# Two recurrent mixers woven on five engines: their steps re-cut so that few wait inside a step, with decays and inverse roots computed on ScalarE

## What is computed

```python
# mixer A (hgrn2), 6 heads of 64: per head, over time
G = cumsum(log_f)
o = (q * exp(G)) @ state + scores @ v         # scores: q k^T with decays exp(G_t - G_s), causal
state = exp(G_last) * state + (k * exp(G_last - G))^T @ v
y_a = rms_norm(o) * norm_w * silu(g)          # rms over the 64 of a head
# mixer B (mamba2), 6 heads of 64, 2 groups of state 128: per chunk
a_cum = cumsum(dt * a)
scores = (c b^T) * exp(segsum(dA))            # the decays of a chunk
y = scores @ xdt + exp(a_cum) * (c @ state) + d_skip * x
y_b = rms_norm(y * silu(z)) * norm_w          # rms over 192
```

## Time and profile before

| | us |
|---|---|
| median of 3 runs | 3358.85 (3358.09 to 3359.83) |
| profiled execution, its time | 3351.59 |
| its span | 3349.8 |
| the stage of both mixers, from the first fetch of their inputs (430.16) to the first product of the next stage (755.34) | 325.2 |

### The profile page before, as it was taken

How to read it: one execution, slowest core, us unless ns; L and a number is a source line. 1 busy time by engine, 2 the same in 40 slices (tenths; PEclk the granted TensorE clock), 3 DMA queues, 4 the chain that set the end, 5 groups by cost and what they waited for, 6 DMA issues and landing times.

```text
span 3349.8 us, 36089 instructions
## 1 busy us (share of the span) xinstructions
PE 3054.7 (91%) x15301; PEld 2515.5 (75%) x15301; DVE 1443.1 (43%) x2170; ACT 836.1 (25%) x1123; POOL 794.3 (24%) x513
## 2 busy tenths in 40 slices
PE   8889945569999999999999999799999999999997
PEld 7768745557788888887977889766667878787785
DVE  4766437755433333335235254411125433434335
ACT  3211233321221111111237222311111322322221
POOL 0342312231321112123311255300212211111113
PEclk9989956669999999999999999999999999999998
DMA  4212120113111111111201200211120111111111
GB/s 137 58 54 76 42 77 26 51 57 120 51 51 51 38 51 51 51 40 36 99 26 39 70 7 21 82 38 38 34 105 26 51 51 38 51 51 38 51 51 76
DMA packets 152513, 180.47 MB, mean 54 GB/s; under 512 B 6352, under 2 KB 127888, under 8 KB 152352
## 3 DMA queue, kind: packets, MB, share of 16 engines
q1 hardware_dynamic: 143680, 166.51, 15.9%
q10 hardware_dynamic: 8672, 11.65, 1.0%
HBM read 158.05 MB, written 20.09 MB: 53 GB/s over the span
## 4 chain that ended last, share of the span: by engine, by line
PE 77%; DVE 11%; POOL 4%; ACT 3%; issue 2%; DMA 2%; SPq 0%; ACTq 0%; DVEq 0%; POOLq 0%
PE bank L127 76%; DVE f L158 5%; POOL f L158 4%; DVE f L166 2%; PE bank L142 2%; DVE f L175 1%; ACT f L147 1%; DVE r L158 1%; DVE f L163 1%; ACT r L150 1%; DMA f<-gr_s 1%; DVE f L184 1%; ACT f L150 1%; DMA f<-x 0%; DMA f<-w_in 0%
## 5 line engine op out<-in xcount | busy, mean ns | idle before, releaser
L127 PE MATMUL bank<-r,r 128*128 128x512 f32 (+4 forms) x11592 | 2448.1, 372 | 46.1 <-DVE r L158 23.3
L127 PEld LDWEIGHTS bank<-r,r 128*128 128x128 f32 x11592 | 2017.3, 189 | 467.4 <-issue 51.8
L158 POOL TENSOR_TENSOR f<-f 128x512 f32<-128x512 f32 (+4 forms) x278 | 365.0, 1319 | 1791.3 <-ACT f L147 614.9
L158 DVE TENSOR_TENSOR f<-f,bank 128x512 f32<-128x512 f32 (+2 forms) x519 | 318.4, 635 | 450.7 <-PE bank L127 449.1
L158 DVE TENSOR_TENSOR r<-f,r 128x512 fp32r<-128x512 f32 (+3 forms) x169 | 227.6, 1354 | 511.1 <-ACT r L150 511.1
L127 PE MATMUL bank<-f 128*128 128x128 f32 (+8 forms) x2344 | 343.0, 316 | 103.3 <-DVE f L158 54.2
L127 PEld LDWEIGHTS bank<-f 128*128 128x128 f32 (+3 forms) x2344 | 295.4, 211 | 135.8 <-issue 65.5
L150 ACT ACTIVATE r<-f 128x2048 fp32r<-128x2048 f32 (+2 forms) x217 | 278.8, 1308 | 431.3 <-DMA f<-w_up 181.7
L166 DVE SCALAR_TENSOR_TENSOR f<-f,f 128x1024 f32<-128x1024 f32 (+2 forms) x153 | 196.4, 1288 | 347.5 <-ACT f L147 319.3
L147 ACT ACTIVATE f<-bank 128x512 f32<-128x512 f32 (+1 forms) x187 | 96.6, 518 | 932.7 <-PE bank L127 929.0
L158 POOL TENSOR_TENSOR r<-f,r 128x2048 fp32r<-128x2048 f32 (+1 forms) x48 | 219.7, 4578 | 443.6 <-ACT r L150 443.6
(11 more groups left out here) (31 smaller groups left out, 552.2 us busy)
## 6 DMA issues: line engine op xcount, KB each, us to landing
f<-w_in SPq DMA_DIRECT2D x31, 1024.0 KB, 6.7
f<-w_up SPq DMA_DIRECT2D x44, 512.0 KB, 5.2
f<-w_mlp_in SPq DMA_DIRECT2D x16, 1024.0 KB, 5.5
f<-w_mlp_out SPq DMA_DIRECT2D x16, 1024.0 KB, 4.9
f<-w_down SPq DMA_DIRECT2D x11, 1024.0 KB, 5.0
f<-w_out SPq DMA_DIRECT2D x8, 1024.0 KB, 5.5
f<-x_spill SPq DMA_DIRECT2D x4, 2048.0 KB, 11.7
f<-x SPq DMA_DIRECT2D x4, 1024.0 KB, 11.7
```

The source lines that it names most:

```text
L127: return self.g.matmul(out, lhs, rhs, start=start, stop=stop, skip_group_check=True)
L158: return self.g.tensor_tensor(out, a, b, op)
```

## The change

In `act_*`, `dve_*`, `pool_*`, `pe_*` and `sp_*` of both mixers:

- decays of mixer B: six ScalarE Relu with the column as bias and one Exp per three, in place of six VectorE `ts` and the Exp
- inverse roots, both mixers: ScalarE Ln (scale 1/n, bias eps) and Exp (scale -0.5), in place of VectorE `ts` and POOL `pow`
- skip term: a product of the identity with `XSD` (128x384) opens the bank that the six `diag` products add to, in place of a POOL sum; the product with `ZS` goes to VectorE, and the product with the norm weight joins VectorE's scaling (two `stt` of 128x192)
- `KD`: nine ScalarE Exp with the last column of `G` as bias, in place of two VectorE subtractions and one Exp
- level 3 into `SM`: 8 ScalarE copies a pair in place of 2 VectorE picks
- the pair's end: output products of both halves in two steps on end, outputs copied to SBUF by ScalarE first, roots and transposes a step behind
- steps: two chunks take 7 steps, a chunk's pieces stand a step apart where one engine feeds another; the last work stands in the stage's 34th step instead of its 36th
- loads: `xb_s`, `ac_s` and `z_s` each wait only for the last reader of their own buffer, and each has its own semaphore.

```diff
@@ act_hgrn @@
-        g.wait_ge(*k.past("kd diff", i))
-        g.act(KD, KD, ACT.Exp, scale=-1.0).then_inc(*k.up("hgrn acts", "kd exp", i))
+        for c in range(9):
+            lo, n = (0, NM) if c == 0 else (NM + 128 * (c - 1), 128)
+            ins = g.act(KD[:, lo:lo + n], G[:, lo:lo + n], ACT.Exp, scale=-1.0, bias=G[:, lo + n - 1:lo + n])
+        ins.then_inc(*k.up("hgrn acts", "kd exp", i))
...
-            if s in (2, 3):
+            if s in (2, 3, 4):
...
+        def root(h):
+            g.wait_ge(*k.past("squares", i, h))
+            g.act(S.RS[h], S.SS[h], ACT.Ln, scale=1.0 / 64, bias=k.eps).then_inc(*k.up("hgrn acts", "rs ln", i, h))
+            g.wait_ge(*k.past("rs ln", i, h))
+            g.act(S.RS[h], S.RS[h], ACT.Exp, scale=-0.5).then_inc(*k.up("hgrn acts", "rs", i, h))
...
@@ pe_hgrn @@
+        outputs(0)
+        yield
+        outputs(1)
+        yield
+        turned(0)
+        yield
+        turned(1)
@@ sp_ssd @@
-        chunk_left(k, g, r - 2)
-        g.dma(S.XBC[x][:, :, 0:n], dr["xb_s"][:, :, lo:lo + n]).then_inc(*k.land(f"chunk in {x}", "chunk in", r, 0))
+        if r == 2:
+            g.wait_ge(*k.past("bt", 0))
+        elif r > 2:
+            g.wait_ge(*k.past("off", r - 2))
+        g.dma(S.XBC[x][:, :, 0:n], dr["xb_s"][:, :, lo:lo + n]).then_inc(*k.land(f"xbc in {x}", "xbc in", r))
         if r:
-            g.dma(S.ZS[x], dr["z_s"][:, r - 1, :]).then_inc(*k.land(f"chunk in {x}", "chunk in", r, 1))
...
+            if r > 2:
+                g.wait_ge(*k.past("diag", r - 2))
             g.wait_ge(*k.past("ac stored"))
             g.dma(S.E[x], dr["ac_s"][r - 1:r, :].to_broadcast([128, 768])).then_inc(*k.land(f"rows in {x}", "rows in", r))
+            if r > 2:
+                g.wait_ge(*k.past("y", r - 2))
+            g.dma(S.ZS[x], dr["z_s"][:, r - 1, :]).then_inc(*k.land(f"z in {x}", "z in", r))
@@ pe_ssd @@
         g.wait_ge(*k.past("xdt", r))
+        g.wait_ge(*k.past("xsd", r))
+        g.mm(bd[:, 0:384], k.ident, S.XSD[x], True, False)
         for h in range(6):
-            ins = g.mm(bd[:, 64 * h:64 * h + 64], S.E[x][:, 128 * h:128 * h + 128], S.XDT[x][:, 64 * h:64 * h + 64])
+            ins = g.mm(bd[:, 64 * h:64 * h + 64], S.E[x][:, 128 * h:128 * h + 128], S.XDT[x][:, 64 * h:64 * h + 64], False, True)
@@ act_ssd @@
+                for h in range(3 * e, 3 * e + 3):
+                    o = E[:, 128 * h:128 * h + 128]
+                    ins = g.act(o, o, ACT.Relu, scale=-1.0, bias=v["AC"][:, 6 * r + h:6 * r + h + 1])
...
+                g.act(o, o, ACT.Exp, scale=-1.0).then_inc(*k.up("ssd acts", "decay", r, e))
...
+        g.act(SS, SS, ACT.Ln, scale=1.0 / 192, bias=k.eps).then_inc(*k.up("ssd acts", "y rs ln", r))
+        g.wait_ge(*k.past("y rs ln", r))
+        g.act(SS, SS, ACT.Exp, scale=-0.5).then_inc(*k.up("ssd acts", "y rs", r))
@@ dve_ssd @@
-                g.ts(o, o, AC[:, 6 * r + hh:6 * r + hh + 1], 0.0, SUB, MIN).then_inc(*k.up("ssd vec", "diff", r, hh))
...
-        g.wait_ge(*k.past("y squares", r, 1))
-        g.ts(SS, SS, 1.0 / 192, RMS_EPS, MUL, ADD).then_inc(*k.up("ssd vec", "y rs0", r))
+        g.wait_ge(*k.past("z in", r))
+        g.tt(y, y, S.ZS[x], MUL).then_inc(*k.up("ssd vec", "y", r))
         yield
         g.wait_ge(*k.past("y rs", r))
-        g.tt(y2, y2, bc(SS, [128, 2, 192], 2), MUL).then_inc(*k.up("ssd vec", "scaled", r))
+        for e in range(2):
+            es = slice(192 * e, 192 * e + 192)
+            g.stt(y[:, es], y[:, es], S.SSB[x][:, e:e + 1], P["m2_norm_w"][:, es], MUL, MUL).then_inc(
+                *k.up("ssd vec", "normed", r, e))
@@ pool_ssd @@
-        g.tt(y, y, S.XSD[x], ADD).then_inc(*k.up("ssd pool", "y0", r))
...
-        g.tt(y, y, S.ZS[x], MUL).then_inc(*k.up("ssd pool", "y", r))
...
-        g.tt(S.SSB[x], S.SSB[x], k.mhalf.to_broadcast([128, 2]), ALU.pow).then_inc(*k.up("ssd pool", "y rs", r))
...
-        g.tt(y, y, P["m2_norm_w"], MUL).then_inc(*k.up("ssd pool", "normed", r))
```

More of the change, by code:

```diff
@@ L326, in __init__ @@
         self.ring = [R.take(SLOT) for _ in range(4)]
-        self.mhalf = R.take(16)[:, 0:1]
+        self.mhalf, self.eps = [v[:, i:i + 1] for v in [R.take(16)] for i in range(2)]
         self.small = R.sub(1022)
@@ L1077, in __init__ @@
         self.MK = k.lnw[:, 0:TM]
-        self.EGL, self.SS, self.RS = sm.take(9), sm.take(8), sm.take(8)
+        self.EGL, self.SS, self.RS = sm.take(9), [sm.take(8) for _ in range(2)], [sm.take(8) for _ in range(2)]
         names = "DT DA AC AL EA EL DS x1 x2 x3 x4"
@@ L1134, in one @@
                 k.o1.load(g, n)
-        for _ in range(8):
+        for _ in range(7):
             yield
@@ L1185, in one @@
         KD, KD3 = S.T, S.KDT.rearrange("p (c n) -> p c n", c=9)
-        for _ in range(3):
+        for _ in range(2):
             yield
@@ L1248, in one, with outputs @@
         S3 = ST.rearrange("p (c n) -> p c n", c=8)
-        for h in range(2):
+        def outputs(h):
             bb = []
@@ L1281, in act_hgrn @@
     c_done(k, g)
+    g.wait_ge(*k.past("half"))
     def one(i):
@@ L1443, in one, with squares, gated @@
             yield
[L1444 to L1453, removed]
+        OU = [G[:, half_slice(h)] for h in range(2)]
+        def squares(h):
+            g.wait_ge(*k.past("sq", i, h))
+            g.rsum(S.SS[h], S.SQ.rearrange("p (n d) -> p n d", d=64)).then_inc(*k.up("hgrn vec", "squares", i, h))
+        def gated(h):
             g.wait_ge(*k.past("rs", i, h))
@@ L1529, in sp_ssd, with fetch @@
     c_done(k, g)
-    g.wait_ge(*k.past("drain", "ac turned"))
-    g.dma(dr["ac_s"].rearrange("c (h t) -> (c h) t", h=6), S.ACT).then_inc(*k.land("ac out", "ac stored"))
-    yield
-    def one(r):
+    def fetch(r):
         x = r % 2
@@ L1587, in one @@
             ins.then_inc(*k.up("ssd products", "bt", r))
-            yield
+        yield
+        yield
+        if r:
+            b, freed = k.take("ssd", B, "cb", r)
+            for f in freed:
+                g.wait_ge(*f)
+            for e in range(2):
+                ins = g.mm(b[:, 128 * e:128 * e + 128], XB[:, 3 + e, 0:n], XB[:, 5 + e, 0:n])
+            ins.then_inc(*k.up("ssd products", "cb", r))
+        if r < 8:
             g.wait_ge(*k.past("drain", "bt", r))
@@ L1601, in one @@
         yield
-        yield
-        b, freed = k.take("ssd", B, "cb", r)
-        for f in freed:
-            g.wait_ge(*f)
-        for e in range(2):
-            ins = g.mm(b[:, 128 * e:128 * e + 128], XB[:, 3 + e, 0:n], XB[:, 5 + e, 0:n])
-        ins.then_inc(*k.up("ssd products", "cb", r))
-        yield
         bd, freed = k.take("ssd", B, "diag", r)
@@ L1666, in one @@
             return
-        for e in range(2):
-            yield
-            o = S.E[x][:, 384 * e:384 * e + 384]
-            g.wait_ge(*k.past("diff", r, 3 * e + 2))
-            g.act(o, o, ACT.Exp).then_inc(*k.up("ssd acts", "decay", r, e))
         yield
```

156 lines of the change are left out of this document (83 added, 73 removed).

## The result

The change makes the kernel faster: 3319.39 us median (3318.31 to 3322.57) against 3358.47 (3357.61 to 3359.83), ratio 0.9885, 95% interval 0.9868 to 0.9902. That is -39 us; the forecast was -58, to 3301, in a range of 3270 to 3338. The profiled run took 3319.71 us.

A forecast was written before the change was run, and what follows sets the result against it. Hand-overs inside a step bound the mixers' stage, VectorE having least room. Middle -39, start -8 and end -11 make -58 us: 3293.6 against the profiled 3351.59, with 7.3 added 3301 us median; range 3270 to 3338.

The forecast's parts named there:

- Start: Before the first level's factors: the first pair's keys product runs earlier, factors at 476 us instead of 485, -8 us.
- End: From the last pick to the next stage's first product: 25.3 us instead of 36.3, -11 us.
- The 29.7, 7.0 and 4.7 us go: Middle: VectorE's waits for ScalarE at L163, for POOL and for squares vanish, as these are asked for a step later.
- The gate: Second pair's gate, in the middle: VectorE waits 8 us in place of 2.28, behind ScalarE's root and decays.
- Scores and diag: Middle: VectorE idles 2 us for each of six chunks where TensorE has scores and a diag, 12 us.
- Half of the old waits: Middle: half of VectorE's old waits for TensorE, 14.6 and 5.0 us, stays: 10 us.
- A pair's end: Both halves' output products run ahead of the next pair's first scores, which VectorE needs: 8 us idle for each of two pairs.
- VectorE busy 151: VectorE's work in the middle: net -19 us, leaving 151 us busy of some 197.
- ACT 131 us, two thirds busy: ScalarE in the middle: 77 us plus 54 added, 131 of 197 us, taken as covered.
- ACT couples the steps: Rival: roots, decays and copies share ScalarE's queue; half of its added 54 us shows, +27: 3328 us; chance 0.15.
- TensorE at 1.2 GHz: Rival: TensorE at the lower clock becomes the bound, 213 us in place of 236, in all -42: 3317 us; chance 0.15.
- Drains: Rival: a fixed price behind each of 28 new table loads, all seen, +36 on the forecast: 3337 us; chance 0.02.

The follow-up runs named there:

- e10: Kernel before the change with only the roots moved: ScalarE's Ln and Exp in place of VectorE's mean and GpSimd's power; 3386.92 us, ratio 1.0089.
- e7: Changed kernel with the 48 decay subtractions with a minimum back on VectorE instead of ScalarE's Relu; 3325.81 us, middle 225.6 us.
- e12: Changed kernel with level-3 picks back on VectorE and the skip term added by VectorE instead of the identity product; 3327.92 us, middle 224.8 us.
- e8: Changed kernel with the old condition for a chunk's xb_s load, waiting until the chunk two before has left; 3321.17 us, middle 219.7 us.
- e4: Changed kernel with the newer pair's piece written first on every engine, in three steps at each of two pair ends; 3321.35 us, middle 218.2 us.
- e5: Changed kernel with the newer pair's piece first at the two pair ends, one step earlier than in e4; 3312.41 us, middle 216.6 us.
- e11: Changed kernel with GpSimd roots, newer pair first, its first score products ahead of the older pair's output products, w_out loads later; 3303.62 us, middle 207.7 us.
- e9: Changed kernel with unread products of constants added ahead of TensorE's waits for keys and last picks, to raise its clock; 3325.59 us, ratio 0.9904.
- e2: Changed kernel with the roots' Ln made an Identity, so 28 table loads fewer and norms not the reference's; 3313.27 us, middle 208.1 us.
- e3: Changed kernel with the roots' power on GpSimd after a ScalarE Identity, no table loads for them; 3307.62 us, middle 207.2 us.

## Why the prediction was right, and where it was off

The direction, the range and the two ends of the stage were right, and the mechanism too: the hand-overs inside a step are what was removed. The size was 19 us too large, all of it in the middle.

- *Start*, -8 forecast: -10. *End*, -11: -12. The first level's factors came at 474.4 (476 forecast), the next stage's first product at 716.5 (697 forecast).
- *The 29.7, 7.0 and 4.7 us go:* yes, but for the squares at a pair's end, which came back larger. e10 shows that the roots' new engine does not do this: with the roots alone the kernel loses 30 us. The other parts that were undone are worth 7.3, 6.5 and 1.4 us of the middle (e7, e12, e8), which leaves the new steps; no run has them alone.
- *The gate*, 8 us: 7.6. *Scores and diag*, 12 us: the picks wait 9.1. *Half of the old waits*, 10 us: 6.6 for TensorE's products of mixer B, 2.2 for other first scores and 4.3 for ScalarE.
- *A pair's end, 8 us for each of two:* this term was mis-sized. The sums wait 13.4 (5.4 and 8.0) and the new pair's masks 3.4 + 2.2 + 4.5 + 1.3 = 11.5: 24.9 instead of 16. I counted one wait of VectorE for TensorE's chain; it stops in front of that chain twice. That the three other orders that were tried shorten it by 2 us at most is shown (e4, e5, e11). That the lower clock makes it long is in part argued: outputs take 6.74 us in the earlier trace rows against 4.78 for the same 32 products at 692.43 and 4.2 in e9, but no run has the pair ends at the higher clock without added products.
- *VectorE busy 151:* 160.2. What goes was sized well: 15.8 for the subtractions, 3.8 for the picks (28.5 to 24.7), 2.7 for KD (128x1024: 24.7 to 22.0) and some 2 for the small instructions. What comes was not: I gave 4.2 us. By the groups, the scaling in two pieces takes 5.2 (409 ns each, where I took half of 0.55 and a start), and the other 128x384 instructions grew from 49 in 29.4 us to 55 in 34.3. The 42 level differences (64x512) grew from 32.9 us to 35.4. Part of that are collisions, under "What I had not expected".
- *ACT 131 us, two thirds busy:* 135.7 of 218. A Relu has 388 ns recorded where I took 300, but three start and end within 0.97, 0.32 each. 28 more loads (85 in the trace, 57 before), each followed at once by an Activate: yes, but for the one at 562.05, behind which the Activate waits 3.2 us for VectorE's sum.
- *ACT couples the steps* was the rival nearest the truth in mechanism: half of its added 54 us seen would have given 3328. The loads alone are seen with 10 of 36 us (e2, e3); the other 18 us of added work were not taken out, except for the Relus, and there VectorE's own work weighed more (e7). I had them at nothing in the sum but for the gate.
- *TensorE at 1.2 GHz*, 3317, came nearest in time, which is luck: its bound was not what held. It took the clock at 0.5 throughout, and the middle has 0.74 with TensorE busy 135 of 218 us; TensorE still waits 38.6 us for VectorE there, and e12 takes products off TensorE and is slower.
- *Drains*: no gap behind a load (489.39 + 1.28, then 490.68), and without the 28 loads 10 us are won in the middle, less than the loads' own 36. The Trainium skill, "ScalarE: Activation LUTs", section "What ACT_TABLE_LOAD costs", adds 1.38 us to each; the trace of this kernel shows no such gap behind the new loads, the wait for VectorE at 562.05 apart.

## What to carry to other kernels

Before moving a short dependent operation to an engine with more room, ask what stands in front of it in that engine's queue and what its reader does meanwhile: the same root on ScalarE cost 30 us where its reader waited within the step, and 11 where the reader came a step later. When a pair of steps is bound by a chain through two engines, reordering the pieces can merely rename the wait (e5, e11); shortening the chain is what is left to try, and was not tried here. And an engine that was 73% busy passed on 0.70 and 0.87 of each us that it was given (e7, e12), so offloading it pays, but not in full. Last, read small gains from the stage's own rows: the rest of this program moves by 8 us from run to run.

## What I had not expected

VectorE's product of decays and scores and GpSimd's, the other half of the same work, start in the same step, and behind VectorE's half now stands its product that decays the state. That one is held up. The timeline of the changed kernel:

```profile
563.51 0.56 DVE L158 TENSOR_TENSOR f<-f 128x384 f32<-128x384 f32 x1
563.56 1.36 POOL L158 TENSOR_TENSOR f<-f 128x384 f32<-128x384 f32 x1 [23.63 <-DVE f L158]
563.99 1.35 DVE L158 TENSOR_TENSOR f<-f,f 128x384 f32<-128x384 f32 x1
```

and the same product of the state in the kernel before, where it stood in another step and GpSimd had nothing beside it:

```profile
549.51 0.55 DVE L158 TENSOR_TENSOR f<-f,f 128x384 f32<-128x384 f32 x1
```

It takes 1.35 us instead of 0.55, while GpSimd's runs until 564.92. GpSimd's own 1.36 is 1.00 at 494.07, where it starts ahead of VectorE's. All seven products of the state take 1.35 to 1.36 us now, six of them in the middle: 4.8 us. The kernel before had such meetings too, which I had not looked for: of its seven one took 2.70 us, at 527.33 beside a GpSimd product of 128x1024, and two scalings took 1.00 (602.88, 689.58), 3.1 us in its middle. The level differences (64x512, 0.69 us alone) meet GpSimd's products as well: five take 1.1 to 2.8 us now, four took 1.3 to 2.9 before, and this is the 2.5 us by which the group grew. The Trainium skill, "SBUF — State Buffer", section "Terms", says that VectorE and GpSimd share a pair of ports, and that the loser waits for the whole instruction of the other; the rows agree in size (VectorE's starts at 563.99 and ends 0.42 after GpSimd's). No run here took one of the two away.
